# Modulation sums of a diffusion layer: two interleaved VectorE chains, and six more blocks moved from TensorE to VectorE

## The reference

```python
m = (jax.nn.silu(c) @ w_ada[l] + b_ada[l]).reshape(bsz, n_mod, d)       # 1024 -> 9 x 1024, for latent tokens
mc = (jax.nn.silu(c_ctx) @ w_ada[l] + b_ada[l]).reshape(1, n_mod, d)    # the same weights, for context tokens
x = residual_post_norm(x, swiglu(modulate(x, m, 0), ffn1_w_in, ffn1_w_out), m[:, 2], FFN_HALF, ...)
xc = residual_post_norm(xc, swiglu(modulate(xc, mc, 0), ffn1_w_in, ffn1_w_out), mc[:, 2], FFN_HALF, ...)
y, yc = token_mixer(modulate(x, m, 1), modulate(xc, mc, 1), ...)
x = residual_post_norm(x, y, m[:, 5], 1.0, ...)
x = residual_post_norm(x, swiglu(modulate(x, m, 2), ffn2_w_in, ffn2_w_out), m[:, 8], FFN_HALF, ...)
```

## Time and profile before

| | us |
|---|---|
| median of 3 runs | 1434.86 (1434.32 to 1437.18) |
| the profiled execution | 1434.89 |
| its span | 1433.1 |
| TensorE busy | 1382.1 |
| VectorE busy | 739.7 |
| ScalarE busy | 519.2 |

### The profile page before, as it was taken

How to read it: one execution, slowest core, us unless ns; L and a number is a source line. 1 busy time by engine, 2 the same in 40 slices (tenths; PEclk the granted TensorE clock), 3 DMA queues, 4 the chain that set the end, 5 groups by cost and what they waited for, 6 DMA issues and landing times.

```text
span 1433.1 us, 17893 instructions
## 1 busy us (share of the span) xinstructions
PE 1382.1 (96%) x7405; PEld 1148.7 (80%) x7405; DVE 739.7 (52%) x995; ACT 519.2 (36%) x716; POOL 83.0 (6%) x86
## 2 busy tenths in 40 slices
PE   6999999999999999999999999999979999999997
PEld 3777778888789998788777678887769888888885
DVE  6443326566656776553055547667664324333246
ACT  3425212222223456545153335546373222132220
POOL 4000000000000000000011111111000000000000
PEclk9999999999999999999999899999989999999999
DMA  9855455566545665451121111112324321533311
GB/s 302 251 170 177 146 176 162 147 184 186 174 147 148 176 177 160 158 191 40 30 74 45 30 43 47 46 59 94 112 59 118 94 95 62 136 99 89 101 61 59
DMA packets 199104, 172.84 MB, mean 121 GB/s; under 512 B 6362, under 2 KB 166632, under 8 KB 199024
## 3 DMA queue, kind: packets, MB, share of 16 engines
q1 hardware_dynamic: 188968, 133.82, 32.5%
q0 software_dynamic: 9856, 37.78, 7.9%
q10 hardware_dynamic: 200, 0.09, 0.0%
HBM read 169.58 MB, written 2.10 MB: 120 GB/s over the span
## 4 chain that ended last, share of the span: by engine, by line
PE 85%; DVE 7%; ACT 5%; issue 4%; DMA 0%; ACTq 0%; DVEq 0%
PE ps L1707 25%; PE ps L1708 24%; PE ps L1709 24%; ACT w_hi L730 2%; PE ps L2137 2%; PE ps L2135 1%; DVE w_lo L1142 1%; ACT hfull L759 1%; PE ps L1733 1%; PE ps L2120 1%; DVE xl L1210 1%; PE ps L2084 1%; PE ps L1743 1%; PE ps L1752 1%; PE ps L1933 1%
## 5 line engine op out<-in xcount | busy, mean ns | idle before, releaser
L1707 PE MATMUL ps<-h_hi,w_lo 128*128 128x512 f32 (+1 forms) x1120 | 393.9, 352 | 10.8 <-DVE h_lo L1203 5.6
L1708 PE MATMUL ps<-h_lo,w_hi 128*128 128x512 f32 (+1 forms) x1120 | 389.2, 348 | 0.0
L1709 PE MATMUL ps<-h_hi,w_hi 128*128 128x512 f32 (+1 forms) x1120 | 389.1, 347 | 0.0
L1142 DVE TENSOR_TENSOR w_lo<-w_raw,w_hi 128x2048 fp32r<-128x2048 f32 (+2 forms) x110 | 243.5, 2216 | 213.8 <-ACT w_hi L730 213.7
L730 ACT ACTIVATE w_hi<-w_raw 128x2048 fp32r<-128x2048 f32 (+2 forms) x110 | 203.5, 1851 | 355.5 <-PE ps L1709 337.6
L1707 PEld LDWEIGHTS ps<-h_hi,w_lo 128*128 128x128 f32 x1120 | 212.5, 190 | 43.2 <-issue 7.4
L1709 PEld LDWEIGHTS ps<-h_hi,w_hi 128*128 128x128 f32 x1120 | 212.3, 190 | 27.7
L1708 PEld LDWEIGHTS ps<-h_lo,w_hi 128*128 128x128 f32 x1120 | 212.6, 190 | 25.7
L1707 PE MATMUL ps<-h_hi,half_lo 128*128 128x512 f32 (+1 forms) x272 | 103.6, 381 | 0.3 <-issue 0.2
L1708 PE MATMUL ps<-h_lo,half_hi 128*128 128x512 f32 (+1 forms) x272 | 98.5, 362 | 0.0
L1709 PE MATMUL ps<-h_hi,half_hi 128*128 128x512 f32 (+1 forms) x272 | 98.3, 362 | 0.0
(11 more groups left out here) (252 smaller groups left out, 1869.4 us busy)
## 6 DMA issues: line engine op xcount, KB each, us to landing
w_raw<-ffn_w_in SPq DMA_DIRECT2D x132, 512.0 KB, 5.2
ada_block<-w_ada POOLq DMA_DIRECT2D x34, 1024.0 KB, 5.8
w_raw<-ffn_w_out SPq DMA_DIRECT2D x60, 512.0 KB, 4.0
half_raw<-w_mix_in SPq DMA_DIRECT2D x48, 256.0 KB, 3.3
w_raw<-w_mix_in SPq DMA_DIRECT2D x8, 512.0 KB, 4.4
w_raw<-ffn_w_out SPq DMA_DIRECT2D x12, 256.0 KB, 4.2
w_raw<-w_mix_out SPq DMA_DIRECT2D x6, 512.0 KB, 4.9
xl<-x SPq DMA_DIRECT2D x4, 512.0 KB, 5.2
```

The source lines that it names most:

```text
L1142: nc.vector.tensor_tensor(lo, raw, hi.bitcast(F32), ALU.subtract).then_inc(s_lo[s], 1)
L1707: nc.tensor.matmul(dst, s_low, m_high, start=start, stop=False)
L1708: nc.tensor.matmul(dst, s_high, m_low, start=False, stop=False)
L1709: return nc.tensor.matmul(dst, s_high, m_high, start=False, stop=stop)
```

## The change

Blocks 14 to 19 are summed on VectorE too, for both vectors, and the sums run as two chains in turn: `ada_row` has two rows, step n writes row n mod 2 and waits for step n-2 instead of n-1. With two vectors (blocks 14 to 19) there are 16 steps and each row is one vector's sum; with one vector (blocks 20 to 35) there are 8 steps as before, and even and odd k-slices are summed in a row each. TensorE's turn then has four matmuls instead of two: one per half and vector, or two per half that add up the rows. The triangles `tri` move into the unused half of `glu` to make room, and ScalarE's second Silu waits for them.

```diff
-def for_latent_alone(m):
-
-    return m >= 20
+def vectors(m):
+
+    return 1 if m >= 20 else 2
+
+
+def on_vector(m):
+
+    return m >= 14
...
-                ada_row = sb("ada_row", [P, 256], F32, s3)
+                ada_row = sb("ada_row", [P, 2, 256], F32, s3)
...
+        tri = glu[:, 1, 0:2 * P].rearrange("p (a b) -> p a b", b=P)
...
-                if m > ADA_FIRST and for_latent_alone(m - 1):
-                    pool.wait_ge(s_ada_row, m - ADA_FIRST)
+                if m > ADA_FIRST and on_vector(m - 1):
+                    pool.wait_ge(s_ada_row, 2 * (m - ADA_FIRST))
...
+                        if (tag, part, j) == ("L1", 0, 1):
+                            act.wait_ge(s_tri, 1)
...
             def ada_sums(m):
+
+                steps = ([(k, v, v, k == 0) for k in range(KT) for v in range(2)] if vectors(m) == 2 else
+                         [(k, k % 2, 0, k < 2) for k in range(KT)])
                 dve.wait_ge(s_ada_loaded, 16 * (m - ADA_FIRST + 1))
                 dve.wait_ge(s_silu_c, 1)
-                ins = nc.vector.tensor_scalar(ada_row[:, :], ada_block[:, 0, :], c_cols[:, 0, 0:1], None, ALU.mult)
-                for k in range(1, KT):
-                    link(ins)
-                    ins = nc.vector.scalar_tensor_tensor(out=ada_row[:, :], in0=ada_block[:, k, :], scalar=c_cols[:, k, 0:1],
-                                                         in1=ada_row[:, :], op0=ALU.mult, op1=ALU.add)
-                ins.then_inc(s_ada_row, 1)
+                first = own[0]
+                for n, (k, row, v, begins) in enumerate(steps):
+                    if n >= 2:
+                        dve.wait_ge(s_own, first + n - 1)
...
+                    if n < len(steps) - 2:
+                        own[0] += 1
+                        ins.then_inc(s_own, 1)
+                    else:
+                        ins.then_inc(s_ada_row, 1)
...
             def ada_turn(m):
-                pe.wait_ge(s_ada_row, m + 1 - ADA_FIRST)
-                if for_latent_alone(m):
+                pe.wait_ge(s_ada_row, 2 * (m + 1 - ADA_FIRST))
+                if on_vector(m):
                     pe.wait_ge(s_ones, 16)
                     pe.wait_ge(s_ada_out, m - ADA_FIRST)
                 for j in range(2):
-                    ins = nc.tensor.matmul(ada_ps[:, j, :], ada_row[:, j * P:(j + 1) * P],
-                                           ones[:, 0:2] if for_latent_alone(m) else quad_sum[:, :], start=True, stop=True)
+                    c = slice(j * P, (j + 1) * P)
+                    if not on_vector(m):
+                        ins = nc.tensor.matmul(ada_ps[:, j, :], ada_row[:, 0, c], quad_sum[:, :], start=True, stop=True)
+                    elif vectors(m) == 2:
+                        for v in range(2):
+                            ins = nc.tensor.matmul(ada_ps[:, j, v:v + 1], ada_row[:, v, c], ones[:, 0:1], start=True, stop=True)
+                    else:
+                        for row in range(2):
+                            ins = nc.tensor.matmul(ada_ps[:, j, :], ada_row[:, row, c], ones[:, 0:2], start=row == 0,
+                                                   stop=row == 1)
                 ins.then_inc(s_ada_turned, 1)
```

More of the change, by code:

```diff
@@ L1158, in ada_take @@
                 dve.wait_ge(s_ada_done, m + 1 - ADA_FIRST)
-                nc.vector.tensor_copy(ada_row[:, :], ada_row_ps).then_inc(s_ada_row, 1)
+                nc.vector.tensor_copy(ada_row[:, 0, :], ada_row_ps).then_inc(s_ada_row, 2)
             def ada_out(m):
                 dve.wait_ge(s_ada_turned, m + 1 - ADA_FIRST)
-                b, n = ADA_SEQ[m], 1 if for_latent_alone(m) else 2
+                b, n = ADA_SEQ[m], vectors(m)
                 bias = cols[:, 2 * b:2 * b + 2].unsqueeze(2).to_broadcast([P, 2, n])
@@ L1273, in ffn @@
                         i, idx = JOB[tag, "in", part, j], HID[tag, part, j]
-                        if ada_of(i) is not None and not for_latent_alone(ada_of(i)):
+                        if ada_of(i) is not None and not on_vector(ada_of(i)):
                             ada_out(ada_of(i))
@@ L1287, in ffn @@
                         between(tag, b)
-                        if ada_of(i) is not None and for_latent_alone(ada_of(i)):
+                        if ada_of(i) is not None and on_vector(ada_of(i)):
                             ada_out(ada_of(i))
```

9 lines of the change are left out of this document (7 added, 2 removed).

## The result

| | before | after |
|---|---|---|
| median (lowest to highest), us | 1436.67 (1434.32 to 1439.3), 7 runs | 1444.07 (1440.57 to 1446.83), 7 runs |
| ratio to before, 95% interval | | 1.0054, 1.0043 to 1.0066 |
| profiled execution, span | 1433.1 us | 1441.4 us |

What follows compares the result with a forecast made beforehand. TensorE, busy for 96% of the span, was taken as the bound. Terms -7.5 + 9.7 + 12.3 - 1.5 = +13.0, or +12.8 followed through, on 1434.89 gave 1447.7 us; range 1440 to 1457, the forecast's own 1443 to 1453.

Steps and rivals of the forecast that it cites:

- second rival: Blocks 14 to 19: shorter circle of 12.4 us by quicker loads or steps, waits some 6 us; 1441 us, chance 0.18.
- Step 1: Blocks 14 to 19: products taken off TensorE save 1.25 us a block, -7.5 us.
- step 2: TensorE's turns: four passes more cost 0.44 us in each of 22 turns, +9.7 us.
- Step 3: VectorE's sums: two chains give a step every 0.405 us; sixteen steps take 6.3 us, eight 3.05.
- rival without gain: VectorE's sums: steps still cost 0.52 us, sixteen take 8.1; +24 us, 1459 us, chance 0.16.
- Step 4: Blocks 14 to 19: sum and next load make a 13.8 us circle that paces TensorE; waits +12.3 us.
- Step 5: Blocks 20 to 35: shorter sums cause no wait and remove job 28's wait, -1.5 us.
- Step 6: ScalarE's new wait for the triangles ahead of a Silu is covered by 4.6 us: nothing.
- third rival: Blocks 14 to 19: no pacing, only job 11 waits, about 1.5 us; +2.2 us, 1437 us, chance 0.06.

Runs made afterwards that it cites:

- e1: Kernel before with two chains and four-matmul turns for blocks 20 to 35 only; blocks 14 to 19 stay on TensorE: 1439.88 us, ratio 1.0020.
- e5: Kernel before with only blocks 15, 16, 18 and 19 moved to VectorE in two chains; 20 to 35 keep one chain: 1434.28 us, ratio 0.9988.
- e9: e8 with no block in the short job 11, blocks 17 to 35 one job later: 1427.53 us, ratio to before 0.9945.
- e4: Changed kernel with every step of the sums waiting for the step ahead: 1456.83 us, ratio to before 1.0142.
- e3: Changed kernel with unread matmuls put ahead of the turns of blocks 14 and 17 to fill TensorE's waits: 1445.31 us, ratio to before 1.0056.
- e2: Kernel before with blocks 14 to 19 on VectorE in two chains; 20 to 35 keep one linked chain and two-matmul turns: 1437.64 us, ratio 1.0016.
- e10: Kernel before's sums, with only the turns of blocks 20 to 35 moved to the middle of the next job: 1432.62 us, ratio 0.9977.
- e8: e2 with the turns of VectorE's blocks moved to the middle of the next job: 1433.53 us, ratio to before 0.9984.

## Why the prediction was right, and where its sizes were off

The direction, slower by over 0.2%, was right, and 1444.07 lies in the forecast's own range of 1443 to 1453. Of the +12.8 us, +7.7 came (+10.5 in L1 by the trace). That it lies in this range is partly luck. Two errors partly cancelled: the waits were put too high, and the clock was left out. And the forecast stands on 1434.89 us, where before's median came out 1.8 us higher; 7.7 us on 1434.89 would have been 1442.6, in the range of the second rival, whose condition (loads in 5.7 us) is the one that came true. That rival's own size is slightly off: with a circle of 12.4 us from 154.6, block 19's sum ends at 216.6 and not at 218, which makes its total about +6 us.

- **Step 1** (-7.5) and **step 2** (+9.7): right. The turn measured 0.81 us against a predicted 0.80, and `e1` holds the sixteen turns of blocks 20 to 35 alone. `e5` and `e9` bear out the gain by the products.
- **Step 3** (a step every 0.405, sixteen in 6.3 us): right, 0.395 and 6.14. `e4` shows that the rival without gain was a real alternative: with the linked pitch the ratio is 1.0142, +20 us (+23.9 in L1), where the rival said +24. The page of the Trainium skill that the prediction sets against the change says in the same section that a next operation that is not held starts earlier; the prediction left this out.
- **Step 4** (+12.3 us of waits) is the term that was mis-sized, and its mechanism held only in part: the waits are 4.5 us, at two turns instead of six. TensorE did not fall to the pace of the circle; the turns of blocks 15, 16, 18 and 19 found their sums done, and job 14 started at 221.07 and not near 224.5 (job 8 only 1.0 us earlier than in before). I took 7.1 us for a load beside the main weights, and it is 5.8 and 5.7; the circle is 12.3 us, not 13.8. A tenth of a microsecond was to be worth 0.5 us of the time, and this accounts for 7.5 us. The second rival had put the waits at some 6 us. Block 14's wait, 1.22 us against 1.4, has nothing to do with the circle: its sum is too long for the end of job 8. The longest wait is at job 11, as predicted, but the reason given for it is not what holds there: the load issued at 180.85 should, with 5.75 us, have landed by 186.6, while the sum began at 187.21, right behind `L1305` and `L1185` on VectorE, with no wait for a load. There the sum waits for its place in VectorE's round, and TensorE's job is too short for it.
- **What step 4 left out**: the granted clock. I charged a wait as idle time alone. Behind both waits the clock fell to 1.2 GHz, which cost 4.9 us. `e3` gave 4.0 us of L1 back by filling the waits with work. Without this term the result would have been near the second rival's.
- **Step 5** (-1.5): right. TensorE has no wait left in 225.30 us. Job 14 to the context is +5.70 by the trace, 16 x 0.44 - 1.5 = 5.5 by the prediction.
- **Step 6** (nothing): in the trace of after, ScalarE's second Silu starts at 66.08 us, right behind its instruction ahead, without a wait. No run tested the step by itself.
- The third rival (no pacing) fell, though `e9` shows one way to get there without a faster sum: a later turn and a free short job.

With the measured sizes: -7.5 + 22 x 0.45 + 4.5 + 4.9 - 1.5 = +10.3, against +10.5 in L1. Open is why the whole time differs by 7.7, 2.8 less. The traces give 1.0 of it to the opening and 1.2 to the clock behind L1, where 4 us come and go with the same instructions. But the 2.8 us stand between medians, outside the ratio's interval, and `e1`, `e2`, `e4` and `e10` lie off to the same side; whether the changed kernels meet fewer falls of the clock there isn't settled.

## What to carry to other kernels

Work taken off the bounding engine has to be in time at the one place where that engine asks for it. Compare the length of the sum itself, from the place where it may start, and the circle of the single buffer (load, issue, use) with the shortest job they must fit into, not with the mean one; where the circle was longer here, a later point of use alone gained 0.7 us of L1 (`e8`), and with the short job left free 6.3 (`e9`). A wait of TensorE can cost twice its length, since the clock may fall behind it: read the granted clock in windows of a few microseconds around each new wait, as a mean over the kernel (0.989 here, in the profiled run) hides it. And compare it with a second trace of the same kernel: a fall may come and go without any change.

## What was not expected of the hardware

- How far the clock falls behind a wait does not go by the length of the wait alone. Behind 1.22 us, with a turn and gate rows behind it (24 small passes), it fell to 0.50. In `e4`, behind 1.83 us (183.86 to 185.92, less 0.23), with the turn's 8 passes and then main products, it did not fall: the turn took 0.91 us and the products came every 0.23. Nor was there a fall behind before's wait of 1.14 us, whose window has 1.00. What each wait is followed by differs in these places, but so does what stands ahead of them; no run varied the one alone.
- The clock also falls with hardly a wait. Some 350 us behind the first context product, TensorE goes through small products (`attT`, `qstate`) in the same order before and after, with 0.17 us of idle time ahead of them. These are its windows of 2 us there in the traces of before and after:

```profile
788.83:790.83 2.00, 2.00 (x7) 0.59 0.93 254
...
798.37:800.37 2.00, 2.00 (x11) 1.00 0.94 246
```

  In the second trace of before it is 0.50. The same instructions thus meet a fall in one execution and none in another. The falls behind the two waits of this change, in contrast, stand in each trace that has these waits (after, `e2`, `e4`).
- Two chains in turn bring VectorE's steps of 128x256 from 0.526 to 0.395 us apart, though a single one's record lasts 0.485: records of successive steps overlap by 0.09 us.
- The 12 traces have 995.0 to 999.1 us for the same stages behind L1, and the granted clock of one 100 us stretch, 0.91 to 0.97, goes with most of it.
